# Moving the weight slabs and the operands of a split-precision kernel by 64 bytes in SBUF

## What is computed

```python
def swiglu(x, w_gate, w_up, w_down):
    return (jax.nn.silu(x @ w_gate) * (x @ w_up)) @ w_down
...
def first_block(...):
    h = rms_norm(x, ffn1_norm[l]);  x = x + 0.5 * swiglu(h, ...)          # width 2816
    h = rms_norm(x, mix_norm[l]);   z = h @ w_in[l] + b_in[l]
    # windowed attention and a chunked mLSTM on the columns of z
    x = x + merged @ w_out[l]
    h = rms_norm(x, ffn2_norm[l]);  x = x + 0.5 * swiglu(h, ...)
    return rms_norm(x, final_norm)
def second_block(...):
    # gated linear attention, latent attention, w_out; cross attention on mem; a third
    # feed-forward with a 3-tap convolution on its gate
```

## Time and profile before

| | |
|---|---|
| median of 3 runs | 991.72 us |
| the 3 runs | 982.53, 991.92, 991.72 us |
| profiled execution, its time | 990.06 us |
| profiled execution, span of its instructions | 988.3 us |
| TensorE MATMUL / LDWEIGHTS busy | 977.0 us / 960.1 us |
| VectorE, ScalarE, GpSimd busy | 685.8, 535.6, 124.7 us |
| mean granted TensorE clock | 0.997 of full speed |

### The profile page before, as it was taken

How to read it: one execution, slowest core, us unless ns; L and a number is a source line. 1 busy time by engine, 2 the same in 40 slices (tenths; PEclk the granted TensorE clock), 3 DMA queues, 4 the chain that set the end, 5 groups by cost and what they waited for, 6 DMA issues and landing times.

```text
span 988.3 us, 20534 instructions
## 1 busy us (share of the span) xinstructions
PE 977.0 (99%) x8307; PEld 960.1 (97%) x8307; DVE 685.8 (69%) x1062; ACT 535.6 (54%) x775; POOL 124.7 (13%) x81
## 2 busy tenths in 40 slices
PE   8999999999999999999999999999999999999998
PEld 7999999998999999999999999989899999999998
DVE  4767657467879969767676656586577487888752
ACT  6554454445558955355444465376666565455441
POOL 0111110100035000012111102300001022222200
PEclk9999999999999999999999999999999999999999
DMA  7775585455554545575655664345235445666762
GB/s 242 245 201 188 185 263 175 145 172 169 165 178 133 166 129 171 171 255 173 197 183 170 216 221 145 100 128 169 86 128 172 128 140 159 204 194 196 234 205 72
DMA packets 169085, 172.33 MB, mean 174 GB/s; under 512 B 5685, under 2 KB 166975, under 8 KB 168895
## 3 DMA queue, kind: packets, MB, share of 16 engines
q1 hardware_dynamic: 169006, 171.45, 54.6%
q10 hardware_dynamic: 16, 0.00, 0.0%
HBM read 170.39 MB, written 1.06 MB: 173 GB/s over the span
## 4 chain that ended last, share of the span: by engine, by line
PE 97%; ACT 1%; DVE 1%; DMA 1%; POOL 0%; issue 0%; SPq 0%; DVEq 0%
PE acc L718 86%; PE part L763 1%; PE acc L763 1%; PE part L799 1%; DMA xraw<-in_x 1%; PE part L823 1%; PE part L1095 1%; PE part L809 1%; PE part L1116 1%; PE part L1294 0%; PE part L843 0%; PE part L1085 0%; PE part L881 0%; PE part L1276 0%; PE part L910 0%; PE part L1105 0%
## 5 line engine op out<-in xcount | busy, mean ns | idle before, releaser
L448 ACT ACTIVATE wh<-raw 128x1024 fp32r<-128x1024 f32 (+2 forms) x292 | 317.8, 1111 | 281.3 <-PE acc L718 130.1
L467 DVE TENSOR_TENSOR wl<-raw,wh 128x1024 fp32r<-128x1024 f32 (+2 forms) x294 | 391.1, 1370 | 55.5 <-ACT wh L448 52.8
L718 PE MATMUL acc<-ah,wh 128*128 128x256 f32 x1520 | 427.2, 281 | 0.5 <-DVE xT L2023 0.2
L718 PE MATMUL acc<-ah,wl 128*128 128x256 f32 x1520 | 423.1, 278 | 0.0
L718 PE MATMUL acc<-al,wh 128*128 128x256 f32 x1520 | 423.1, 278 | 0.0
L718 PEld LDWEIGHTS acc<-ah,wh 128*128 128x128 f32 x1520 | 286.2, 188 | 4.3 <-issue 3.4
L718 PEld LDWEIGHTS acc<-ah,wl 128*128 128x128 f32 x1520 | 287.1, 189 | 0.0
L718 PEld LDWEIGHTS acc<-al,wh 128*128 128x128 f32 x1520 | 286.0, 188 | 0.1
L2730 POOL TENSOR_TENSOR sil<-sil,rstd 128x512 f32<-128x512 f32 x33 | 61.6, 1866 | 311.0 <-ACT sil L1407 219.6
L718 PE MATMUL acc<-hh,wh 128*128 128x256 f32 x352 | 97.6, 277 | 0.0
L718 PE MATMUL acc<-hh,wl 128*128 128x256 f32 x352 | 97.4, 277 | 0.0
(11 more groups left out here) (433 smaller groups left out, 1527.3 us busy)
## 6 DMA issues: line engine op xcount, KB each, us to landing
raw<-in_ffn_w_up SPq DMA_DIRECT2D x33, 1024.0 KB, 5.3
raw<-in_ffn_w_down SPq DMA_DIRECT2D x24, 1408.0 KB, 6.4
raw<-in_w_in SPq DMA_DIRECT2D x33, 1024.0 KB, 5.3
raw<-in_ffn_w_gate SPq DMA_DIRECT2D x32, 1024.0 KB, 5.3
raw<-in_w_out SPq DMA_DIRECT2D x8, 1024.0 KB, 5.1
raw<-in_w_proj_attn SPq DMA_DIRECT2D x4, 1024.0 KB, 5.7
raw<-in_w_proj_mlstm SPq DMA_DIRECT2D x4, 1024.0 KB, 5.3
raw<-in_xa_w_kv SPq DMA_DIRECT2D x4, 1024.0 KB, 5.2
```

What stands on the lines that cost most here:

```text
L448: nc.scalar.activation(wh[:, slot, a * nw:b * nw], raw[:, slot, a * nw:b * nw], ACT.Copy).then_inc(S("w_hi"), 1)
L467: nc.vector.tensor_tensor(wl[:, slot, a * nw:b * nw], raw[:, slot, a * nw:b * nw], f(wh[:, slot, a * nw:b * nw]), SUB).then_inc(S("w_lo"), 1)
L718: ins = mm(dst, a, b, start=st and q == 0, stop=en_ and q == 2, skip_group_check=True)
```

## The change

```diff
         raw = sb("raw", [P, 2, SLAB])
-        half = sb("half", [P, 16])
+
         wh = sb("wh", [P, 2, SLAB], f32r)
         wl = sb("wl", [P, 2, SLAB], f32r)
-        rest = sb("rest", [P, 16])
+        rest = sb("rest", [P, 48])
         xT = sb("xT", [P, DC, T])
```

## The result

The changed kernel takes 1003.91 us (median of 6 runs, 1000.46 to 1005.16) against 987.07 us of the kernel before on the same chip (6 runs, 981.41 to 991.92). The ratio is 1.0161, with a 95% interval from 1.0122 to 1.0199: slower by 1.6%.

What follows compares the result with a forecast made beforehand. TensorE, busy 99%, was taken as the bound through its products' pace: 976 us all fast plus 14 us of slow pace gives 990; splits, DMA and small products added nothing. Likeliest 990 us, 8-in-10 range 975 to 1008.

Steps and rivals of the forecast that it cites:

- the two paces: TensorE's long product streams: the same instructions run at 113.4 ns (fast) or 117.8 ns (slow), 4.4 ns a matmul apart.
- (1): ScalarE and VectorE splits, wh now at raw's remainder: at most 0.3 us, hidden under the products, so nothing.
- (2): DMA transfers, with the loads of x and the constants on the path: 0, with 1 us on both sides.
- (3): TensorE's small products, some 800 matmuls outside L718 and L763, reading at shifted places: taken as 0.
- One sign that was to speak against the whole forecast: Granted clock below 1.00 in the products; listed with a third pace and waits on wl of several us.
- The swap of the two forms: Large products: moving minus stationary, +192 plain and -192 tokens, swaps modulo 512; slow marks of 281 and 279 ns would swap.
- Rival C: Large products get on better at the new places: 976 us if the slow pace goes, down to 960; chance 0.22.
- A: Redraw: the shift only shuffles fast and slow stream starts; likeliest 990 us, range 982 to 1000; chance 0.47.
- B: Plain form inherits the tokens form's mostly slow starts: 1002 us, with all slow 1009; chance 0.27.
- the plain form: Products with the stationary side at 192, the moving side at 384; 2,750 of 6,360 counted slow, 43%.
- the tokens form: Products with the stationary side at 384, the moving side at 192; 480 of 1,020 counted slow.
- The upper end: Large products' upward bound: all slow, +19 us, 1009 us; a third, slower pace not excluded, but none occurs.

Runs made afterwards that it cites:

- The map: Also called the coarse map: 64 pairs of stationary and moving places, transposes and product streams only, no kernel work; fast starts 15 of 24 at 192, 2 of 24 at 320.
- One half of the change alone: Kernel before with only the weights moved, 192 to 128, operands staying at 384: 1022.75 us, ratio 1.0318.
- the two maps that differ at one start: The 64-pair map and the next; stationary at 0, moving at 192, four transposes: slow in the first, fast in the next, where another stream came before.

## Why the prediction was wrong

**What bounds the kernel, the two paces, their price: right.** Only the pace of the products changed, by 4.4 ns between 113.4 and 117.8, and parts (1), (2) and (3) came out at nothing, as costed: the 5 ns more of a split are hidden. One sign that was to speak against the whole forecast did turn up, a granted clock below 1.00 in the products, but for 1.6 us of the profiled execution only.

**The swap of the two forms: right.** The marks of 281 and 279 ns and the starts of the two forms changed places, and three arrangements that keep a distance but not the places (992 us with that of before, 1004 with that of the change, 991 with that of before plus 256) show that it is the distance, with a period of 256 bytes. (Rival C had reckoned modulo 512.)

**The choice of A over B: wrong, and it is the step that failed.** The section on the rivals had B's sum at 1002 us, from the starts of the two forms. The profiled execution took 1001.14, the median is 1003.91. Yet B got 0.27 and A 0.47, on the ground that "few of the starts compare" and that a start hangs on a hair's breadth of timing. The second, which no run settles, does not carry: a draw may be decided by a hair and still have odds, and the odds went with the distance. A kept the odds of before, 43% of the plain form slow; 81% of it is. The map, where all distances have the same hooks, gives 15 fast of 24 at 192 and at 448, and 2 of 24 at 64 and at 320. The evidence stood in the trace of before: 3 fast of 19 in the tokens form, where A says one in two. With fair draws that do not depend on one another, 3 or fewer of 19 have a chance of (1 + 19 + 171 + 969) / 524,288 = 0.2%. I set the confounding hooks against it without asking how strong they would have to be, and the pair of the earlier trace rows, same hook and other form, pointed B's way.

**That B's sum fits to a microsecond is luck in part.** Its 84% of the plain form slow was near (81%), but the tokens form, taken as half slow, came out at 15%. B has 5,850 slow products in all, against 5,320: 530 x 4.4 ns = 2.3 us too many. The 1.6 us at the lower clock, which no rival had, make up for most of it.

**The upper end: right for this distance only.** "A third, slower pace can't be excluded by a row, but none occurs" held for the change, since the distances 192 and 320 are the only ones in it. One half of the change alone would have left the range, at 1022 us with a pace of 120.0 ns that no row of before showed.

**C: no.** The all-fast kernel of 976 us did not turn up at any distance, nor did a stream below 113.3 ns.

**What stays open.** Which small difference decides a start at 192 is not settled. The three starts of the coarse map repeat exactly when the moving tensor is 256 bytes further on, so they are not chance in that kernel; the two maps that differ at one start suggest that what came before a stream has a part in it. The time of the real one differs from run to run (984 to 1003 us); that its starts draw otherwise then is likely and not shown, since each kernel has one trace. What in SBUF or in TensorE makes the distance count was not tried; the experiments show the dependence and not its circuit.

## What to carry to other kernels

Where TensorE is the bound and its weight loads alone come nearly as slowly as the pairs with matmuls (here 111.3 ns apart against 113.4), read the pace, starts per microsecond, and not only its busy share; where one trace has two paces of the same instruction, count how often each form or place starts in which, and forecast from that count. Then treat the distance between the moving and the stationary operand modulo 256 bytes as a parameter (shown for fp32r matmuls of 256 columns; no other shape or type was tried), move both sides together when something must be moved, and don't change one pad without working out the distance that it leaves. When a change swaps two roles that the trace of before already shows, take each role's record over to the other and give it most of the chance.

## What the runs showed of the hardware

The pace of pairs of a matmul with 256 moving fp32r columns and an LDWEIGHTS of 128 depends on the distance of their two operands modulo 256 bytes: 113.3 or 117.8 ns a pair at 192, mostly 117.8 at 64, mostly 118.7 at 128, 120.0 at 0, and 120.1 or 122.1 at 196. In the kernel that is 3.2% for 64 bytes of padding (ratio 1.0318). The pace holds through a thousand matmuls, with VectorE, ScalarE and DMA at work or without them (the maps run with none), and in the traces of the kernels it changes only where the stream breaks off or its form changes.

The Trainium skill, "SBUF — State Buffer", section "Who interferes with whom", has TensorE's two read ports independent and TensorE waiting on no one; by it all these kernels would take the same time. The runs here differ by 3.2% through addresses alone, so the measurement decides: other engines indeed don't show in the pace, which is 113.3 ns with them and without, but where the two operands of TensorE itself lie relative to each other does.
